# A two-layer trunk with a mixture of experts: router turned round, first token list made early, gates laid on expert rows, final norm by token row

## The reference

```
x = x + g_m * (concat(y_first, y_second) @ w_out[l])
h = rms_norm(x, norm_gain[l, 1]) * (1 + sc_f) + sh_f
scores = sigmoid(h @ w_router)            # 16 experts in 4 groups
# best group by its two best biased scores, two best experts in it,
# gate = their scores over the sum of both
out[token] = sum over the two: gate * ((silu(xb @ w_gate[e]) * (xb @ w_up[e])) @ w_down[e])
x = x + g_f * out
...
return rms_norm(x, final_gain)            # after the last layer
```

## Time and profile before

| | us |
|---|---|
| three runs | 1763.6, 1764.68, 1770.03 (median 1764.68) |
| the profiled execution | 1767.98 |
| its span | 1766.2 |
| TensorE busy in it | 1503.6 (85%) |
| VectorE, ScalarE, GpSimd busy | 645.3, 326.4, 74.5 |
| mean granted TensorE clock | 0.907 |

### The profile page before, as it was taken

How to read it: one execution, slowest core, us unless ns; L and a number is a source line. 1 busy time by engine, 2 the same in 40 slices (tenths; PEclk the granted TensorE clock), 3 DMA queues, 4 the chain that set the end, 5 groups by cost and what they waited for, 6 DMA issues and landing times.

```text
span 1766.2 us, 22612 instructions
## 1 busy us (share of the span) xinstructions
PE 1503.6 (85%) x9877; PEld 788.9 (45%) x9877; DVE 645.3 (37%) x1055; ACT 326.4 (18%) x516; POOL 74.5 (4%) x201
## 2 busy tenths in 40 slices
PE   5999999858877976999996699987569679999964
PEld 2445555447664453333332345663434533333323
DVE  1124342257763143222221535535741432222224
ACT  2121211233331020111110212213110201111103
POOL 7000000000000000000001000000000000000020
PEclk9999999969998977999998699978779679999986
DMA  9687561030000086999976410210000869999761
GB/s 335 206 275 246 190 216 51 11 134 3 3 28 24 0 333 238 417 376 357 424 278 264 179 48 25 90 53 0 1 1 0 332 251 426 371 367 423 278 259 65
DMA packets 91264, 334.71 MB, mean 190 GB/s; under 512 B 6441, under 2 KB 37405, under 8 KB 74781
## 3 DMA queue, kind: packets, MB, share of 16 engines
q1 hardware_dynamic: 76160, 285.32, 42.3%
q10 hardware_dynamic: 8956, 25.91, 3.7%
q0 software_dynamic: 6048, 22.02, 3.3%
HBM read 310.17 MB, written 23.07 MB: 189 GB/s over the span
## 4 chain that ended last, share of the span: by engine, by line
PE 74%; DVE 15%; ACT 5%; DMA 4%; issue 2%; POOL 0%; POOLq 0%; SPq 0%; DVEq 0%; ACTq 0%
PE banks L1556 18%; PE banks L1168 15%; PE banks L1578 9%; PE banks L1498 7%; DVE work L1673 4%; PE banks L1201 3%; PE banks L1157 3%; PE banks L1110 3%; PE banks L1138 2%; DMA work<-in_w_down_dram 2%; PE banks L1539 2%; DVE work L1679 2%; DVE ring L1673 1%; DVE x_features L1679 1%; DMA ring<-in_w_ada_dram 1%
## 5 line engine op out<-in xcount | busy, mean ns | idle before, releaser
L1168 PE MATMUL banks<-h_features,ring 128*128 128x512 f32 (+1 forms) x656 | 293.8, 603 | 4.7 <-ACT h_features L837 4.7
L1556 PE MATMUL banks<-ring,work 128*64 128x512 f32 x672 | 231.0, 606 | 2.2 <-ACT work L1023 2.2
L1556 PE MATMUL banks<-work 128*64 128x512 f32 x512 | 212.3, 595 | 0.0
L1168 PEld LDWEIGHTS banks<-h_features,ring 128*128 128x128 f32 (+1 forms) x656 | 122.6, 191 | 159.3 <-issue 155.6
L1673 DVE TENSOR_TENSOR work<-work,banks 128x256 f32<-128x256 f32 (+1 forms) x86 | 43.7, 531 | 259.4 <-PE banks L1556 205.8
L1498 PE MATMUL banks<-y_features,ring 128*128 128x512 f32 x256 | 115.2, 614 | 8.6 <-DVE small L2154 8.6
L1578 PE MATMUL banks<-work 128*64 128x512 f32 x320 | 112.7, 593 | 0.0
L1673 DVE TENSOR_TENSOR work<-work 128x512 f32<-128x512 f32 (+10 forms) x205 | 103.3, 504 | 14.4 <-ACT work L988 3.6
L1556 PEld LDWEIGHTS banks<-ring,work 128*64 128x64 f32 x672 | 70.4, 139 | 79.5 <-issue 74.8
L1578 PE MATMUL banks<-ring,work 128*64 128x512 f32 x256 | 98.4, 592 | 0.0
L1676 DVE TENSOR_SCALAR work<-work 128x512 f32<-128x512 f32 (+5 forms) x54 | 21.4, 396 | 190.8 <-ACT work L1028 124.2
(11 more groups left out here) (334 smaller groups left out, 1913.9 us busy)
## 6 DMA issues: line engine op xcount, KB each, us to landing
ring<-in_w_up_dram SPq DMA_DIRECT2D x16, 2048.0 KB, 12.7
y_features<-in_w_ada_dram SPq DMA_DIRECT2D x28, 1024.0 KB, 5.8
work<-in_w_down_dram SPq DMA_DIRECT2D x14, 2048.0 KB, 14.7
ring<-in_w_gate_dram SPq DMA_DIRECT2D x12, 2048.0 KB, 8.8
work<-in_w_up_dram SPq DMA_DIRECT2D x10, 2048.0 KB, 13.4
work<-in_w_gate_dram SPq DMA_DIRECT2D x10, 2048.0 KB, 12.5
ring<-in_w_ada_dram SPq DMA_DIRECT2D x8, 2048.0 KB, 12.3
h_features<-in_w_gate_dram SPq DMA_DIRECT2D x8, 2048.0 KB, 8.8
```

Source lines behind the costliest of these rows:

```text
L1168: ins = mm(PS[0:w, b, :], lhsT=W[:, k, c0:c0 + w], rhs=h[:, k, :], start=(k == 0), stop=(k == KD - 1))
L1556: ins = mm(PS[rows, bank, :], lhsT=xt[:, k, rows], rhs=ws[lane][:, k, :], start=(k == 0), stop=(k == KD - 1))
```

## The change

Per layer, after the output projection: VectorE adds the squares of the 8 pieces, one add behind each piece, and TensorE multiplies the sum by ones once. The router takes the 16 columns of w_router as the stationary operand and h as the moving one, 8 matmuls of 512 columns; ScalarE takes exp of the 16 x 512 result, and TensorE turns that back in four pieces. The token rows are stored in four DMAs of 512 KB, each behind its copy. The list of round 0 is made by itself: the first 64 tokens of experts 0 and 1, straight from the ranks, so that GpSimd can gather round 0 without the table. The other lists are made by TensorE inside round 0, between gate and up, and the turning of round 1's rows moves behind the up part of round 0. The number of passes is loaded after the 11 rounds by TensorE, ScalarE and GpSimd.

g_f is spread once per layer into gate_row (8 small matmuls and a copy); VectorE in place of ScalarE takes banks 5 and 6 out, times gate_row. So the combination adds a whole tile in one instruction. ScalarE does the first scaling. In layer 0 it squares each tile, TensorE sums the squares tile by tile, and norm(2) is left with its second half. In layer 1 xT is turned into rows while the last store and the gathers are under way, and all the rest is done by token row, with final_gain spread over the partitions by a DMA; SyncE stores the rows. Five semaphores of the layer 1 mixer are replaced by others that count on; no work changes there.

```diff
             def norm(n):
+                if n in (1, 3):
+                    pe.wait_ge(sem("squares_summed"), (KD - 1) * (n // 2 + 1))
+                    mm(PS[:, 6, :], lhsT=ones, rhs=h[:, 0, :], start=True, stop=True).then_inc(sem("ms_ready"), 1)
+                    return
+                if n == 2:
+                    return
...
-                for t in range(NT):
-                    for k in range(KD):
...
-                        ins = mm(PS[:, 4, t * E:(t + 1) * E], lhsT=h[:, k, t * P:(t + 1) * P], rhs=wr[:, k, :],
-                                 start=(k == 0), stop=(k == KD - 1))
+                for k in range(KD):
+                    pe.wait_ge(sem("h_ready"), KD * (2 * l + 1) + k + 1)
+                    ins = mm(PS[0:E, 4, :], lhsT=wr[:, k, :], rhs=h[:, k, :], start=(k == 0), stop=(k == KD - 1))
...
+                pe.wait_ge(sem("rows_copied"), NT * l + NT - 1)
+                for k in range(KD):
+                    ins = mm(PS[:, k // 4, (k % 4) * P:(k % 4 + 1) * P],
+                             lhsT=mod[:, l, 40 + k:41 + k].to_broadcast([P, P]), rhs=ident, start=True, stop=True)
+                ins.then_inc(sem("comb_turned"), 1)
+                pe.wait_ge(sem("choices_ready"), 3 * l + 2)
+                for t in range(NT):
+                    ins = mm(PS[:, 7, 0:1], lhsT=ohf[:, 2 * t:2 * t + 2, :].rearrange("p a b -> p (a b)"),
+                             rhs=tokid[:, t:t + 1], start=(t == 0), stop=(t == NT - 1))
...
                     if r:
                         lanes_down(r - 1, weights(2, r - 1), r - 1 if r > 1 else None)
-                    turn_x((r + 1) % 2, 16 * ((r + 1) // 2 + 1))
+                        turn_x((r + 1) % 2, 16 * ((r + 1) // 2 + 1))
+                    else:
+                        tokens_of_blocks()
                     lanes_up(1, weights(1, r), xTb[r % 2], range(KD)).then_inc(sem(f"l{l}_up_done"), 1)
+                    if r == 0:
+                        turn_x(1, 16)
...
+                pe.wait_ge(sem("table_ready"), l + 1)
+                passes = passes_of(pe, l)
...
# GpSimd
-                pool.wait_ge(sem("table_ready"), l + 1)
-                pool.wait_ge(sem(f"l{l}_rows_stored"), 16)
-                passes = passes_of(pool, l)
+                pool.wait_ge(sem(f"l{l}_rows_stored"), 16 * NT)
+                pool.wait_ge(sem("first_rows_known"), l + 1)
...
+                    if r == 1:
+                        pool.wait_ge(sem("rows_known"), l + 1)
...
# VectorE, in a round, between the product with bank 0 and that with bank 1
+                def y_out(r):
...
+                    dve.wait_ge(sem(f"l{l}_down_done"), r + 1)
+                    dve.wait_ge(sem(f"l{l}_rows_stored"), (r + NT) * 16)
+                    tt(yb.rearrange("p (a b) -> p a b", a=2), PS[:, 5:7, :], gate_row, ALU.mult)\
+                      .then_inc(sem(f"l{l}_y_copied"), 1)
...
# VectorE, combination of layer 1
+                    def normed(t):
+                        dve.wait_ge(sem("rstd_ready"), 2 * DEPTH + t + 1)
+                        c0 = cg[:, 2 * t, :]
+                        signal(stt(c0, c0, row_scale[:, t:t + 1], gain_row.rearrange("p a b -> p (a b)"), ALU.mult,
+                                   ALU.mult), "combined")
+
+                    for t in range(NT):
+                        link(weigh(t))
+                        dve.wait_ge(sem("comb_turned"), (NT + 1) * l + t + 2)
+                        c0 = cg[:, 2 * t, :]
+                        signal(tt(c0, c0, PS[:, 2 * t:2 * t + 2, :].rearrange("p a b -> p (a b)"), ALU.add), "comb_added")
+                        if t:
+                            normed(t - 1)
+                    normed(NT - 1)
```

248 lines of the change are left out of this document (157 added, 91 removed).

## The result

The changed kernel took 1726.24 us in the median of four runs (1720.86 to 1726.72), the kernel before 1767.36 (1763.6 to 1774.98) beside it. The ratio is 0.9749, 95% interval 0.9727 to 0.9772: 44 us faster, between 40 and 48. The profiled execution took 1720.86, its span is 1719.1, against 1767.98 and 1766.2: 47.1 less. The forecast for it was 53 less.

A forecast was written before the change was run, and what follows sets the result against it. TensorE was taken to bound the rounds, but in the stretches between them not to be the bound or to run at half clock. Terms of -17.5 (layer 0) and -35.4 (layer 1) made -53 us: median 1712, range 1697 to 1724.

The forecast's parts named there:

- rival with a router at half clock: Router ahead of the choice: stays on half clock and takes 13.8 us, 5.6 more per layer, 1723; chance 0.13.
- fast-gather rival: Round 0: second gather lands within 6.3 us of its issue, 6.8 less per layer, 1698; chance 0.22.
- Norm and router: Each layer up to the choice: one ones matmul and a router of 16 rows in 9.1 us, -8.5 us.
- Choice to first gather: From the choice to round 0's gather: the early list brings it forward, -10.4 us in layer 0, -9.4 in layer 1.
- It moves no term, as the list comes later than the stores: Row stores ahead of the first gather: the split costs nothing, rows stored at 652.7, gather at 654.4.
- late-rows rival: Row stores: go one behind another and land at 680, so the early list brings nothing, 1763; chance 0.03.
- Round 0: First gather to round 1's gate: second gather lands late, TensorE idles, +10.1 us in layer 0, +10.6 in layer 1.
- This gives back half of what the early list gained: Remark on round 0: its +10.1 us returns half of the early list's gain.
- Rounds 1 to 11: Rounds to the last y store: VectorE's output step costs nothing, 22.67 us each; +1.0 in layer 0, +0.7 in layer 1.
- Combination: Layer 0's combination, work spread over VectorE, ScalarE and TensorE: -9.7 us, bounds -5.0 and -11.0.
- End: End of layer 1, x turned during the gathers and the rest done by token row: -28.8 us.
- warning signs: Signs of being wrong: rounds grow longer, TensorE waits for weight loads in rounds 1 to 3, second gather far from 11.

The follow-up runs named there:

- e3: Changed kernel with round 0's two 2 MB down-weight loads held back until the first gather has landed; 1724.2 us, ratio 0.9728 to the kernel before.
- e4: Changed kernel with SyncE's weight loads from home 6 on held back until the second gather has landed; 1721.1 us, ratio 0.9706 to the kernel before.
- e10: Changed kernel without the first list, both gathers behind the full lists and gate_row's rows behind those; 1717.7 us, ratio 0.9674 to the kernel before.
- c0: Changed kernel run once more, unedited, as the control in a later group; 1725.6 us, ratio 0.9720 to the kernel before.
- e11: Changed kernel with full lists in round 0's gate part, down weights held back, gate_row behind first list, layer 0's four scalings ahead of squares; 1705.5 us, ratio 0.9605.
- e2: Changed kernel with the full lists' 32 rows put inside round 0's gate part instead of behind it; 1709.0 us, ratio 0.9637 to the kernel before.
- e9: Changed kernel with its four 512 KB row stores put back into one of 2 MB; 1720.6 us, ratio 0.9702 to the kernel before.
- e12: Changed kernel with full lists in round 0's gate part, down weights held back, gate_row's rows ahead of the ranks; 1700.8 us, ratio 0.9599.
- e1: Changed kernel with the first list computed but unused, first gather waiting for all lists, built ahead of round 0; 1728.3 us, ratio 0.9764.
- e8: Changed kernel with the old router of 64 products, exp on the token side, nothing turned back; 1733.9 us, ratio 0.9767 to the kernel before.

## Why the prediction held, and where it was off

The forecast was faster, 1712 within 1697 to 1724, against a median before of 1764.68. By the ratio (0.9749 of 1764.68) the result is 1720: the sign holds, and so do the mechanisms of the norm, the router, round 0, the combination and the end. The gain was taken 9 us too large (53 for 44); the profile's 47.1 is nearer only by the 3.3 of layer 1's mixer. 1720 lies in the range, but just outside the 1704 to 1719 that had a chance of 0.58. It is nearest to the 1723 of the rival with a router at half clock, which did not happen: the number alone would have pointed to the wrong cause. The ends of the range are not the sum of the bounds named with it, either: these give 8.2 down and 10.8 up, 1704 to 1723, and the 1697 is there for the fast-gather rival. What made the 9 us: the first gather (2.9 and 3.1), round 0 (0.7 and 0.6), the combination (0.9), the matmul with ones in layer 1 (0.9), the end (0.5); the rounds gave 0.5 back.

- **Norm and router**: as forecast in layer 0. The ones matmul ends at 622.3 (622.2), the router takes 9.47 (9.1), the choice begins at 636.33 (636.4). The rival of a router at half clock is out. In layer 1 the ones matmul took 2.07, not the 1.0 that the forecast took for both layers.
- **Choice to first gather** is the term that failed. The list's copy was nearly right: it ended 18.3 behind the choice's first step, forecast 17.6 (the 18.0 is to the gather). "It moves no term, as the list comes later than the stores" was wrong. The fourth store was issued at 641.3, near the 642 taken, but the stores take 12.3 and not 10.7 in the median, and the last landed nearly 16 behind its issue, since they end with the 12 MB of weights issued ahead of them: 2.5 and 3 per layer. e3 shows the cause. The argument that refuted the late-rows rival took all bytes together and had them through "by 654", later than the 652.7 of the term itself; even that was 3 too early. Of the time up to the list, 1.5 went to the ranks, forecast 4.3 and measured 5.8 on half clock; gate_row's rows and the list gave 0.5 of that back.
- **Round 0**: +10.8 and +11.2 for +10.1 and +10.6. Landing 11.3 (11.1), idle 5.0 (4.8), round 1's gate part 10.6 from its start at 689.96 to its exp, against 8.0 where it ran warm (697.92 to 705.89 before), 2.6 (2.0). The fast-gather rival is out for a reason that e4 prices: 5.2 alone, 11.3 beside the loads. The Trainium skill (DMA: Bandwidth & Descriptors, Queues, rings and completion order) says that each DMA engine goes round between the queues packet by packet; it does not say that the bytes are shared evenly. If they were, two gathers of 512 KB would have had half of 423 GB/s and landed in some 5 us (an estimate), which is not what the row shows.
- "This gives back half of what the early list gained" was arithmetic against its own sum: -10.4 and +10.1 cancel. The two terms stood in different paragraphs, and I never asked what the early list was worth by itself. As placed it gained nothing: with list and gate_row's place changed, e10 is 6.6 us faster. The 1.2 per layer that turning the second rows behind the up part costs was in the sum, as part of its 2.4, and went as unquestioned.
- **Rounds 1 to 11**: 22.67 each (exp of rounds 1 and 2 at 700.57 and 723.24), VectorE's y_out hidden, the down weights a wait of 1.3 in layer 0 and 1.8 in layer 1 (before, 2.2 for both layers together). **Combination**: root 24.8 behind the first tile, forecast 23.5, and 23.2 in c0. The last 32 matmuls of the sums of squares took 5.42 in the one, with the clock at 0.72 over 982 to 988, and 3.84 in the other, with 1.00: the miss is the clock. The fourth scaling stood behind two squares, but e11 shows that this order alone does not set the time. **End**: 28.3 for 28.8; ScalarE's scaling takes 1.15, not 1.0.
- The warning signs named were the right ones: the second gather was near 11, and TensorE did not wait for weights in rounds 1 to 3.

## What to carry to other kernels

When a first item is made ready early so that work can start, write down when the second item must be there, and add the two terms before believing either: here a first list 8 us earlier bought a stall and a half clock that cost as much or more. Making the full lists inside the first item's own work gained 5 to 8 us per layer on that (e2), which leaves round 1 some 2 to 5 us earlier than without the early list (e10). Here row stores issued behind 12 MB of weights landed when these did, as four of 512 KB and as one of 2 MB (e9), and sooner with 4 MB held back (e3); look for the idle DMA stretch behind such transfers and move there what is due last. A reordering that takes one wait away should be read at the end of the stage, not at the wait (e3, e4, e11 and e12 all moved their wait and changed little or nothing at the end). And a run that changes two things prices neither: e10 took the list out and moved gate_row, and only e1 beside it shows how much may be the list's.

## What was not expected of the hardware

- The same instructions in the same order kept TensorE's clock in one layer and not in the other (e12: ranks 3.3 and 5.6, granted clock 0.88 in 646 to 652 and 0.78 in 1364 to 1370). Idle time ahead of them was 1.6 in both. So with the one matmul with ones: in layer 1 it ran on half clock (1.93 to 2.07) in 12 of 13 profiles of the changed kernel and its variants, in e9 on full clock (1.12); in layer 0 it took 1.12 or 1.13 in 12 of 13, and 2.00 in e8. The idle time ahead of it was 2.37 in all.
- Code that the change does not touch moved the choice between 636.6 and 646.7 from one execution to another; in the two that were compared TensorE's granted clock in the mixer differed, 1.00 against 0.93 and 0.90. What makes the clock differ there stays open.
- A 512 KB gather took 5.2 with no loads beside it and 11.3 beside 2 MB loads, with the next gather behind it in both.
